# Prompt attention: the next tile's index scores go beside the second attention's logits, and GpSimd sums them

## The reference, cut to what matters

```python
def indexer_scores(qi, wi, ki):      # 8 index heads of 64
    dots = jnp.einsum('bqhd,bkd->bqhk', qi, ki) * IDX_DIM ** -0.5
    return jnp.einsum('bqhk,bqh->bqk', jax.nn.relu(dots), wi * IDX_HEADS ** -0.5)

def select_topk(scores, admissible, k):                      # k = 256
    vals, idx = lax.top_k(jnp.where(admissible, scores, -jnp.inf), k)
    return idx, jnp.isfinite(vals)
# A: softmax(qa . ka over the selected keys) @ va            8 heads, one key head
# B: softmax(qb . kb + c_q - c_k over keys <= query) @ vb    8 heads, two key heads
```

## Time and profile before

| | us |
|---|---|
| median of 3 runs | 4882.49 (4882.02 to 4884.57) |
| the profiled execution, its own time | 4881.96 |
| its span in the trace | 4880.3 |
| first to last logits of the prompt attention on DVE | 642.8 to 2409.0 |

### The profile page before, as it was taken

The page is one execution under the profiler, slowest core; times in us unless marked ns, Lnnn a source line. Parts: engine busy times, 40 slices in busy tenths (PEclk is TensorE's granted clock), DMA queues, the critical chain, the costliest instruction groups (busy, mean ns, idle before and its releaser), DMA issues. The chain is left out here.

```text
span 4880.3 us, 62248 instructions
## 1 busy us (share of the span) xinstructions
PE 4193.3 (86%) x23550; PEld 3176.2 (65%) x23550; DVE 2684.0 (55%) x4986; ACT 1770.7 (36%) x2709; POOL 608.2 (12%) x695
## 2 busy tenths in 40 slices
PE   7999847777788787888887789797999999999997
PEld 3444424445555555555545544587999999999997
DVE  2222149989999999999423311463335353353533
ACT  2332223444444454544443344312323233233331
POOL 0212221100000000000076741000000000000000
PEclk9999957778888898899989888898999999999998
DMA  3322221000000000000086762344444544445442
GB/s 132 103 81 98 92 89 32 25 23 16 16 16 16 16 10 16 7 16 1 11 276 196 216 234 73 117 133 123 126 120 132 142 112 126 121 129 140 118 127 68
DMA packets 460724, 444.90 MB, mean 91 GB/s; under 512 B 26728, under 2 KB 405299, under 8 KB 460484
## 3 DMA queue, kind: packets, MB, share of 16 engines
q1 hardware_dynamic: 403396, 256.46, 18.5%
q0 software_dynamic: 57104, 185.42, 11.3%
HBM read 371.71 MB, written 69.95 MB: 90 GB/s over the span
## 5 line engine op out<-in xcount | busy, mean ns | idle before, releaser
L467 DVE TENSOR_SCALAR_CACHE_REDUCE at_relu<-at_scores,at_cand 128x272 f32<-128x272 f32 (+14 forms) x480 | 685.2, 1427 | 9.4
L1484 PE MATMUL ff_ps<-ff_h_high,ff_w_high 128*128 128x412 f32 x1760 | 619.6, 352 | 25.6 <-DVE ff_w_low L1578 25.6
L1485 PE MATMUL ff_ps<-ff_h_low,ff_w_high 128*128 128x412 f32 x1760 | 615.9, 350 | 0.0
L1486 PE MATMUL ff_ps<-ff_h_high,ff_w_low 128*128 128x412 f32 x1760 | 613.5, 349 | 0.0
L306 PE MATMUL pP<-w_in,hT 128*128 128x500 f32 x1088 | 469.0, 587 | 30.7 <-ACT hT L354 19.0
L1578 DVE TENSOR_TENSOR ff_w_low<-ff_w_raw,ff_w_high 128x2048 fp32r<-128x2048 f32 (+1 forms) x150 | 375.7, 2505 | 189.8 <-ACT ff_w_high L1533 189.7
L921 ACT ACTIVATE at_probs<-at_probs,at_nmax 128x144 f32<-128x144 f32 (+15 forms) x256 | 311.2, 1216 | 461.9 <-DVE at_nmax L1003 461.7
L1533 ACT ACTIVATE ff_w_high<-ff_w_raw 128x2048 fp32r<-128x2048 f32 (+1 forms) x150 | 311.7, 2078 | 360.2 <-PE ff_ps L1486 357.8
L934 ACT ACTIVATE at_pT_sb<-tr 128x512 f32<-128x512 f32 x544 | 304.6, 593 | 330.8 <-PE tr L807 330.2
L787 PE MATMUL S<-at_kbT,at_queries_b 73*128 73x512 f32 (+16 forms) x768 | 312.5, 549 | 116.3 <-DVE at_nmax L1003 65.3
L306 PEld LDWEIGHTS pP<-w_in,hT 128*128 128x128 f32 x1088 | 203.6, 191 | 262.8 <-issue 260.1
(11 more groups left out here) (318 smaller groups left out, 6624.1 us busy)
## 6 DMA issues: line engine op xcount, KB each, us to landing
ff_w_raw<-in_w_gate SPq DMA_DIRECT2D x110, 512.0 KB, 4.0
ff_w_raw<-in_w_up SPq DMA_DIRECT2D x110, 512.0 KB, 5.2
ff_w_raw<-in_w_down SPq DMA_DIRECT2D x80, 704.0 KB, 6.5
out_PN<-pn POOLq DMA_DIRECT2D x17, 1000.0 KB, 6.3
at_q_raw<-dram_QTA SPq DMA_DIRECT2D x124, 128.0 KB, 2.8
x_in<-in_x_rows SPq DMA_DIRECT2D x17, 512.0 KB, 4.0
dram_HN<-x_in POOLq DMA_DIRECT2D x17, 512.0 KB, 7.7
dram_QTA<-qaiT POOLq DMA_DIRECT2D x17, 512.0 KB, 5.5
```

What stands on the lines that cost most here:

```text
L467: return v.tensor_scalar(out, x, cand.bitcast(F32), 0.0, ALU.is_ge, ALU.add, accum_out=cnt)
L1484: pe.matmul(out, w_high[p][:, w], high, start=first, stop=False)
L1485: pe.matmul(out, w_high[p][:, w], low, start=False, stop=False)
L1486: return pe.matmul(out, w_low[p][:, w], high, start=False, stop=last)
```

## The change

- Stretch C goes. After the logits and turns of each head h of groups g = 0 and 1, PE makes the products of one index head, 4 g + h, for tile t + 1, ACT takes their relu, and ACT multiplies them in place by the query's weight (a second ACT instruction per part, with a semaphore `weighted` of its own).
- POOL adds the weighted part to `scores` (`sum_scores`, a TENSOR_TENSOR of two SBUF inputs). DVE does none of it. It waits for the last of these sums after `choose`.
- `ties` becomes memory of its own, so a relu no longer waits for `choose`.
- `unit` now waits for the unit two before it, whatever its kind.
- The third part of a head's logits (tile 15 alone has one) is multiplied after the head's turns. Before, all parts went ahead of them.
- Queries are loaded and split in another order: the index queries of tile t + 2 in tile t, ahead of the attention queries of tile t + 1; at the start the index queries of tile 1 and the index keys come first, and POOL splits the attention queries of tile 0 before it issues the large loads.
- The index of tile 1 is made beside groups 0 and 1 of tile 0, so tile 1's search too is cut into 16 and 16 bits.

```diff
-        ties = relu[:].rearrange("p a b -> p (a b)")
+        ties = sb("ties", [P, TOTAL])
...
             def tile(t):
                 now = before(t)
+                if t + 2 < QT:
+                    wait(sp, q_split, splits(t, 1))
+                    load_raw(t + 2, 0)
+                    wait(sp, acc_done, now["acc"])
+                    load_wi(t + 2, t % 2)
                 if t + 1 < QT:
-                    wait(sp, q_split, t * 4 + 2)
+                    wait(sp, q_split, splits(t + 2, 0) if t + 2 < QT else splits(t, 1))
                     load_raw(t + 1, 1)
...
+            def sum_scores(t):
...
+                k = done["acc"]
+                for h in range(HEADS):
+                    for c, w in spans(width(t)):
+                        k += 1
+                        wait(pool, weighted, k)
+                        if k > 1:
+                            wait(pool, acc_done, k - 1)
+                        pool.tensor_tensor(scores[t % 2][:, c:c + w], relu[:, (k - 1) % 2, 0:w],
+                                           (scores[t % 2] if h else mask_of(t))[:, c:c + w], ALU.add).then_inc(acc_done, 1)
...
             def unit(kind, n, matmuls):
-                if state["kind"] != kind:
-                    state["before"], state["kind"], state["run"] = state["kind"], kind, 0
                 sems = {"ttr": ttr_done, "relu": relu_done}
-                if state["run"] < 2 and "before" in state:
-                    wait(pe, sems[state["before"]], n[state["before"]].at(state["run"] - 1))
-                else:
-                    wait(pe, sems[kind], n[kind].at(-1))
+                if len(state["last"]) == 2:
+                    other, value = state["last"][0]
+                    wait(pe, sems[other], value)
...
                     for h in range(4):
-                        if g < 2:
-                            logits_b(g, h, W, n)
-                        else:
-                            split_products("ttr", q_a[:, 4 * (g - 2) + h, :], ka_high, ka_low, W, n)
+                        parts = spans(W)
+                        now = 2 if h < 3 else len(parts)
+                        products(t, g, h, parts[:now])
                         if g > 0:
                             weigh(share(t + 1, h, 4), W, n, values(g - 1))
                         elif t > 0:
                             weigh(share(t, h, 4), width(t - 1), n, values(3))
-                if t < FIRST_TOPK:
-                    indexer(t)
+                        products(t, g, h, parts[now:])
+                        if g < 2:
+                            indexer(t, 4 * g + h)
...
                     wait(act, acc_done, n["acc"].at(-1))
-                    act.activation(relu[:, b, 0:w], S[b][:, 0:w], ACT.Relu, scale=HD ** -0.5 * HEADS ** -0.5).then_inc(relu_done, 1)
+                    act.activation(relu[:, b, 0:w], S[s][:, 0:w], ACT.Relu, scale=HD ** -0.5 * HEADS ** -0.5).then_inc(relu_done, 1)
                     n["relu"].add()
+                    wait(act, relu_done, n["relu"].at())
+                    act.activation(relu[:, b, 0:w], relu[:, b, 0:w], ACT.Copy, scale=wi[t % 2][:, h:h + 1]).then_inc(weighted, 1)
...
-                        if has_next_scores(t):
-                            index_scores(t + 1)
+                    if g == 2:
+                        wait(v, acc_done, before(t + 1)["acc"])
```

More of the change, by code:

```diff
@@ L649, in searched, with index_units, splits @@
             return (3 * BITS + 1 + CHOOSE_STEPS) * max(0, t + 1 - FIRST_TOPK) + (t >= FIRST_TOPK)
+        def index_units(t):
+            return HEADS * units(t + 1) if has_next_scores(t) else 0
         def before(t):
             b = sum(units(u) for u in range(t))
-            i = sum(HEADS * units(u + 1) for u in range(t) if has_next_scores(u))
+            i = sum(index_units(u) for u in range(t))
             return dict(full=16 * b + i, ttr=16 * b, acc=i)
+        def splits(t, a):
+            return 2 * (2 * t - 1) if not a else 2 * (2 * t + 2 if t < QT - 1 else 2 * t + 1)
         def share(nb, j, parts):
@@ L702, in tile @@
                 if t + 1 < QT:
-                    wait(sp, s_full, now["full"] + 8 * units(t))
+                    wait(sp, s_full, now["full"] + 8 * units(t) + index_units(t))
                     load_b(t + 1)
@@ L734, in split @@
                 pool.tensor_tensor(q[low], q_raw[low], q[low].bitcast(F32), ALU.subtract).then_inc(q_split, 1)
-            split(q_a, 0)
+            def sum_scores(t):
+                done = before(t - 1)
+                if t >= FIRST_TOPK + 2:
+                    wait(pool, ttr_done, done["ttr"])
+                if t == FIRST_TOPK:
+                    wait(pool, mask_here[0], 16)
+                elif t == FIRST_TOPK + 1:
+                    wait(pool, mask_here[1], 16)
+                wait(pool, q_split, splits(t - 1, 1))
+                k = done["acc"]
[7 more added lines that the diff above has]
+                                           (scores[t % 2] if h else mask_of(t))[:, c:c + w], ALU.add).then_inc(acc_done, 1)
+            split(q_i, 0)
             def split_keys(step, k, cols):
@@ L746, in _ @@
             pool.wait_ge(q_split, 2)
-            for k in range(2):
-                split_keys(k, k, slice(0, near))
+            for k in (1, 0):
+                split_keys(1 - k, k, slice(0, near))
+            split(q_a, 1)
             with nc.allow_non_contiguous_dma(reason="rows of 256 and 512 bytes"):
@@ L873, in values, with indexer, products @@
                 return (lambda kb, keys: vb[0:keys, kb, g * HD:(g + 1) * HD]) if g < 2 else (lambda kb, keys: va[0:keys, kb, :])
-            def indexer(t):
+            def indexer(t, h):
                 if has_next_scores(t):
-                    wait(pe, q_split, t * 4 + 4)
-                    wait(pe, k_split, 4 if t < 1 else (6 if t < 2 else 8))
-                    for h in range(HEADS):
-                        split_products("relu", q_i[:, h, :], ki_high, ki_low, width(t + 1), n)
+                    if h == 0:
+                        wait(pe, q_split, splits(t + 1, 0))
+                        wait(pe, k_split, 2 if t < 1 else 6)
+                    split_products("relu", q_i[:, h, :], ki_high, ki_low, spans(width(t + 1)), n)
+            def products(t, g, h, some):
+                if g < 2:
+                    logits_b(g, h, some, n)
+                else:
+                    split_products("ttr", q_a[:, 4 * (g - 2) + h, :], ka_high, ka_low, some, n)
             def tile(t):
@@ L948, in copies, with relus @@
                         state["tb"] += 1
-            def relus(W, n):
+            def relus(t, h, W, n):
                 for c, w in spans(W):
-                    b = n["full"].n % 2
+                    s, b = n["full"].n % 2, n["relu"].n % 2
                     n["full"].add()
@@ L1095, in tile @@
                         logits(W, n, bias, h, turned(t, g - 2) if t > 0 or g >= 2 else 0)
-                if t < FIRST_TOPK and has_next_scores(t):
-                    index_scores(t + 1)
+                        if g < 2 and has_next_scores(t):
+                            n["full"].add(units(t + 1))
             for t in range(QT):
```

94 lines of the change are left out of this document (38 added, 56 removed).

## The result

| | us | against the kernel before |
|---|---|---|
| forecast | 4846 | |
| changed kernel, median of 6 | 4865.54 (4860.64 to 4872.95) | 0.9962 [0.9952, 0.9972] |
| kernel before, same chip, median of 6 | 4883.53 | 1 |
| the same changed kernel again (run e_again), median of 11 | 4872.4 (4860.47 to 4878.78) | 0.9979 [0.997, 0.9988] |
| kernel before, beside e_again, median of 17 | 4883.11 | 1 |

The change gains 18 us in one comparison and 11 in the other, where 36 were forecast: half of it or less. The two together also tell how far one version repeats: some 0.1 to 0.2%, 5 to 8 us. The profiled execution of the changed kernel is its slowest (4872.95 us); that of e_again, its fastest of 11, took 4860.47. I read both.

A forecast was written before the change was run, and what follows sets the result against it. DVE and PE were both taken as near full in A, DVE as bounding B and D. Terms 59 (A) - 33 (B) + 10 (tiles 0 and 1) + 0 gave 36 us faster, 4846 us; range 4780 to 4890.

The forecast's parts named there:

- A, forecast 728: Stretch A with the index work, tiles 2 to 14: 728 us against 787.2 for A and C before, a gain of 59.
- the chain of 8.4 us a head: Stretch A, tile 11: PE, ACT and DVE wait for each other, so one head's period is 8.4 us.
- 2.4% over PE's sum: Stretch A, all tiles: the chain was taken to last 2.4% longer than PE's 711.0 us of work, giving 728 us.
- ACT busy above 80% in A: Stretch A: a sign that would show the forecast, ACT busy more than 80% of the time.
- Rival 3: Stretch A: a longer chain, partly from half-clock starts, cancels the gain; 4865 to 4890 us, chance 0.15 together with another rival.
- B, 33 lost: Stretch B: the last index head's additions on POOL and `choose` on DVE hold each other, 33 us lost of 40.
- Tiles 0 and 1, 10 gained: Start: tile 1 loses its stretch C and 16 search rounds move under a wait; net 10 us gained, ends -5 and +18.
- D, 0: Stretch D keeps its work and order and stays DVE-bound: no change.
- Tile 15, 0: Tile 15, third part after the turns: fills a wait but delays ACT's copies as much; zero, ends -4 and +5.
- L485 beside POOL, nothing in A: Stretch A: POOL's additions can hold DVE's L485, but the chain's slack of 1.8 us a head covers it; cost nothing.
- rival 2: Stretch A: POOL holds DVE's L485, deciding against the change from 0.88 us each; around 4900 to 4980 us, chance 0.15.
- Rival 1: Stretch A packs tighter and the clock stays up: A 644 us, most at 4760 to 4810 us in all, chance 0.20.

The follow-up runs named there:

- e_warm_index: e_start's two edits on the changed kernel, plus a discarded first pass (low part of the keys) on each index product; 4839.93 us, 0.9905 of the kernel before.
- e_warm_both: e_start's two edits on the changed kernel, plus a discarded pass on the index products and on attention A's logits in groups 2 and 3; 4841.2 us, 0.9905.
- e_queries: Changed kernel, but in tile 0 SP issues tile 1's query load for B ahead of its wait for POOL's split; 4863.62 us, 0.996 of the kernel before.
- e_start: e_queries' edit on the changed kernel, and all 32 search rounds of tile 1 beside its own groups 0 and 1; 4860.75 us, 0.995.
- e_noweight: Changed kernel, but ACT's weighting covers 16 columns instead of the whole part; 4859.97 us, 0.994 of the kernel before.
- e_threepass: Changed kernel, but each index product has a third pass, the low part of the keys added once more; 4842.0 us, 0.9913 of the kernel before.
- e_nolast: Changed kernel, but POOL adds the last index head's part over 16 columns alone; 4852.37 us, 0.9926 of the kernel before.

## What the prediction had right, and the step that failed

The direction and the mechanism were right, and so were the two large terms; the forecast time was 20 us too low, inside the range, but that is half of the gain. The step that failed is the term of tiles 0 and 1, which makes 17 to 20 us of the miss.

- **A, forecast 728: right** (724.2 and 720.3). Tile 11 took 68.9 us, forecast 67 to 70, by the chain of 8.4 us a head. Tile 14 took 96.0 and 93.9 where 87 to 90 stood: its chain was worked out from durations at the full clock, and it ran at 0.86 and 0.89. With the clock at 0.94 it takes 90.1, at 1.00 85.6 (e_warm_index and e_warm_both, with a pass more).
- **The total of A is in part luck.** "2.4% over PE's sum" took 711.0 us of PE as a soft floor in A. PE is busy 652.9 there, and 68 us more than before in B, beside `choose`: a part of the work that it had counted in A runs there. By groups of tiles the 2.4% puts tiles 2 to 6 at 188.5 us (PE is busy 184.1 in their A and C before) and tile 14 at 85.0; they took 176.4 and 96.0, and the two errors about cancel. "ACT busy above 80% in A" was wrong (509 of 724 us, 70%): in B ACT is busy 63 us more than before. Rival 3's "half clock on the chain" was a true mechanism, priced too high.
- **B, 33 lost: right in size and in the main in cause** (35.7). Most of it is the additions; 3.5 us in tiles 7 to 13 are the split, which had been costed at nothing in A and stands in B now. The Trainium skill, SBUF — State Buffer, section Who interferes with whom, counts plain tensor_scalar among the operations that can contend, in a 2-port mode, which no row of before showed. The trace of after agrees, though no view tells the mode: so for L503, one input, 11.5 us before and 22.5 now, and for L500 (rows above). The scan (L498) tells nothing on this, though it is as long as before (38.9 us): no pass of POOL stood beside it in the changed kernel.
- **Tiles 0 and 1, 10 gained: wrong, and the step that failed.** 7 to 10 us were lost. The prediction moved tile 1's query load "by about 5" us and called SP's loads "each still a whole tile ahead of use". It was issued 29.9 us later, 15.8 us before its use. The wait ahead of it on SP is for a split on POOL; POOL stands in the additions and the key split by then; and tile 0 is too short to cover that. The waits followed were those of a tile in the middle, not those of tile 0. e_queries moves this one load and gets the 7 to 10 us back, to 107.1 us, which is what the kernel before takes. The 10 us of forecast gain don't come with it. They rested on the stalls of tile 0 lying "under the wait for the same load": with the load in time, tile 0 still ends at 702.3 us (659.7 before), with 10.3 us of waiting for POOL's loads, 6.2 for its last sum and an L485 of up to 3.0 us beside the key split. e_start frees these L485 and gains nothing, so which of the others to cut is open.
- **D, 0: right within what executions differ** (602.1 and 606.3 against 601.2). **Tile 15, 0: right.**
- **L485 beside POOL, nothing in A: right.** 0.29 us in the mean, far from rival 2's 0.88. It hangs on the chain being slow enough: with the weightings cut short (e_noweight) the mean is 0.47 and the small tiles pay.
- **Rival 1** (A at 644, the clock stays up) shows how much lay in the clock: with it at 0.96, A takes 702 (e_threepass and e_warm_both), not 644, since the chain remains.
- **Two readings of the page were off,** without effect on the sum: DVE's nines reach to slice 19, not 17, and PEclk is at 7 tenths in slices 7 to 9.

Open: why A's clock falls in some tiles and not in others (tile 13 0.96, tile 14 0.86 in the same run), and what tiles 0 and 1 would take without POOL's loads and key split in their way.

## What to carry to other kernels

When work moves beside other work, walk the queues of the first and the last tile instruction by instruction: a load behind a wait for another engine's split is harmless in the middle and late at the start. When engines take turns and none is full, look at PE's granted clock before cutting PE's work: try a discarded pass, since less work can be slower. As `choose` shows, two-input passes on DVE and POOL, and DVE's plain passes of one input too, can be overlapped only where one side has slack; beside a DVE-bound stretch POOL's passes cost nearly their full length. Where such a cost depends on what else stands there, taking out one part at a time doesn't tell the parts' shares: sum what each held pass takes more in the trace instead.

## What the runs showed of the hardware that I had not expected

- Leaving out 1 of 2 index passes made the kernel 37 us slower than e_again (4909.6 against 4872.4); adding a discarded one made it 21 us faster than e_start (4839.9 against 4860.8). The granted clock of A went with it: 0.83 with one pass, 0.89 with two, 0.95 to 0.96 with three.
- DVE and POOL hold each other in turn: POOL's two additions took 6.19 us beside `choose` for 3.9 alone, a DVE pass of one input took 2.99 us beside a POOL pass of 3.75 (e_nolast) for 0.97, and a 128x1 operation of DVE waited up to 3.87 us for a POOL pass of 3.96.
